# Decay rows of an mLSTM scan: broadcast by TensorE into PSUM in place of DMA and GpSimd

## The reference

```python
    def step(carry, inp):
        c_prev, n_prev, m_prev = carry
        qc, kc, vc, li, lf = inp
        b = jnp.cumsum(lf, axis=-1)
        log_d = jnp.where(tri, b[..., :, None] - b[..., None, :] + li[..., None, :], -jnp.inf)
        m_t = jnp.maximum(b + m_prev[..., None], log_d.max(-1))
        d = jnp.exp(log_d - m_t[..., None])
        inter = jnp.exp(b + m_prev[..., None] - m_t)
        s = jnp.einsum("bhtd,bhsd->bhts", qc, kc) * d
        num = jnp.einsum("bhts,bhsd->bhtd", s, vc) + inter[..., None] * jnp.einsum("bhvd,bhtd->bhtv", c_prev, qc)
        den = s.sum(-1) + inter * jnp.einsum("bhd,bhtd->bht", n_prev, qc)
        h = num / jnp.maximum(jnp.abs(den), jnp.exp(-m_t))[..., None]
        ...
        c_new = decay[..., None, None] * c_prev + jnp.einsum("bhs,bhsv,bhsd->bhvd", w, vc, kc)
```

## Time and profile before

| | before |
|---|---|
| median of 3 runs | 2023.67 us (2020.77 to 2026.71) |
| the profiled execution's own time | 2023.67 us |
| its span, first to last instruction | 2021.1 us |
| TensorE busy (matmul) | 1889.4 us, 93% |
| VectorE busy | 1170.4 us, 58% |
| ScalarE busy | 800.4 us, 40% |
| GpSimd busy | 574.2 us, 28% |
| mean granted TensorE clock | 0.965 of full speed |

### The profile page before, as it was taken

The page is one execution under the profiler, slowest core; times in us unless marked ns, Lnnn a source line. Parts: engine busy times, 40 slices in busy tenths (PEclk is TensorE's granted clock), DMA queues, the critical chain, the costliest instruction groups (busy, mean ns, idle before and its releaser), DMA issues. The chain is left out here.

```text
span 2021.1 us, 33770 instructions
## 1 busy us (share of the span) xinstructions
PE 1889.4 (93%) x7936; PEld 1340.5 (66%) x7937; DVE 1170.4 (58%) x1669; ACT 800.4 (40%) x1083; POOL 574.2 (28%) x692
## 2 busy tenths in 40 slices
PE   6999999997879899889999999999999999999785
PEld 1455458446754365478888888888888888888432
DVE  4753772203875553647538898564965873555166
ACT  0111110203230011247638888564865764555100
POOL 2000000003842220723333333332333332333244
PEclk9999996996989999999999999999999999999898
DMA  9732000001231341258648899572975892674586
GB/s 382 279 134 85 1 0 1 0 0 60 105 138 68 134 156 74 97 210 329 251 169 337 318 359 377 221 283 109 377 293 213 310 387 82 262 278 175 232 371 245
DMA packets 76095, 399.23 MB, mean 198 GB/s; under 512 B 20842, under 2 KB 21002, under 8 KB 56851
## 3 DMA queue, kind: packets, MB, share of 16 engines
q1 hardware_dynamic: 44592, 329.38, 42.2%
q0 software_dynamic: 31456, 69.27, 9.3%
q10 hardware_dynamic: 4, 0.02, 0.0%
HBM read 373.52 MB, written 73.77 MB: 221 GB/s over the span
## 5 line engine op out<-in xcount | busy, mean ns | idle before, releaser
L1708 DVE TENSOR_TENSOR split_weights<-raw_weights,split_weights (+1 forms) x384 | 448.0, 1218 | 26.6 <-ACT split_weights L671 22.9
L671 ACT ACTIVATE split_weights<-raw_weights (+1 forms) x384 | 380.9, 1063 | 9.7 <-issue 8.6
L1247 PE MATMUL psum<-split_weights,split_rows 128*128 (+1 forms) x864 | 347.8, 402 | 0.0
L1249 PE MATMUL psum<-split_weights,split_rows 128*128 (+1 forms) x864 | 337.9, 391 | 0.0
L1248 PE MATMUL psum<-split_weights,split_rows 128*128 (+1 forms) x864 | 336.6, 390 | 0.0
L671 ACT ACTIVATE arena<-psum 128x1024 f32<-128x1024 f32 (+3 forms) x202 | 164.0, 819 | 413.7 <-PE psum L1138 125.2
L671 ACT ACTIVATE split_rows<-psum 128x256 fp32r<-128x256 f32 (+1 forms) x217 | 154.2, 711 | 162.0 <-PE psum L1255 149.8
L1249 PEld LDWEIGHTS psum<-split_weights,split_rows 128*128 128x128 f32 x864 | 162.3, 188 | 35.9
L1248 PEld LDWEIGHTS psum<-split_weights,split_rows 128*128 128x128 f32 x864 | 163.0, 189 | 31.1
L1247 PEld LDWEIGHTS psum<-split_weights,split_rows 128*128 128x128 f32 x864 | 163.1, 189 | 30.1
L1266 PE MATMUL psum<-split_weights,split_rows 128*128 x432 | 168.2, 389 | 2.0 <-ACT arena L671 2.0
(11 more groups left out here) (239 smaller groups left out, 2634.1 us busy)
## 6 DMA issues: line engine op xcount, KB each, us to landing
raw_weights<-in_w_gu SPq DMA_DIRECT2D x64, 2048.0 KB
raw_weights<-in_w_dn SPq DMA_DIRECT2D x64, 1024.0 KB
arena<-pair_rows SPq DMA_DIRECT2D x16, 2048.0 KB, 13.4
arena<-in_w_ada SPq DMA_DIRECT2D x12, 2048.0 KB, 9.3
arena<-in_toks SPq DMA_DIRECT2D x18, 512.0 KB, 9.8
arena<-job_rows SPq DMA_DIRECT2D x16, 512.0 KB, 3.7
arena<-in_w_vog SPq DMA_DIRECT2D x1, 4160.0 KB, 12.7
arena<-in_w_qk SPq DMA_DIRECT2D x1, 4096.0 KB, 17.9
```

The costliest lines, as they stand in the source:

```text
L671: return act.activation(o, i, ACT.Copy)
L1247: mm(bank(3 + p), xk, part(par, 0, 512 * k), start=(k == 0), stop=False)
L1249: ins = mm(bank(3 + p), xl, part(par, 0, 512 * k), start=False, stop=(k == 7))
L1708: tt(cols(wsplit, (1 - par) * (2 * WE) + (WE + 1024 * c), 1024), cols(raw, (1 - par) * WE + 1024 * c, 1024), high, ALU.subtract).then_inc( ...
```

## The change

Ri and Rm are no longer sent through DRAM. TensorE spreads them: a product of a selector of 8 rows with a row block writes the row of one head to all 128 partitions of a PSUM bank. For Rm a product of the identity and the mask goes first into the same bank (2 or 5), in the f32r format, from a tile `maskr` that VectorE copies once. ScalarE's exponentials read that bank. VectorE multiplies q by the spread Ri straight out of bank 6, which is shared with half 1 of `update`; so TensorE writes Ri there only after the state update has read the previous half 1, and issues half 1 only after qI is made. qI is made for the current job, no longer one job ahead. `SD_done` is now given by `masks`, and ScalarE waits for it; GpSimd has no `log_decay`; VectorE no longer waits for scores apart from Dt. The rows for d = 1 are read backwards by TensorE.

```diff
-        bcast = [at(D0 + 1024 * i, 1024).rearrange("p (v h n) -> p v h n", v=2, h=4) for i in range(3)]
-        logd = at(D0 + 3072, 1024).rearrange("p (b h n) -> p b h n", b=2, h=4)
+        maskr = overlay("maskr", HB + 3600, 3 * P, F32R)
 ...
 # SP
-            sp.wait_ge(S("rows_exp"), 5)
-            sp.wait_ge(S("front_dve"), ROWS_REV_0 + 3)
-            for v, r in enumerate((Ri, Rm)):
-                for d in range(2):
-                    sp.dma_start(job_rows[d, :, DM * v:DM * v + DM]..., r[4 * d:4 * d + 4, :]...).then_inc(S("job_rows_out"), 16)
-            sp.wait_ge(S("job_rows_out"), 64)
-            def load_job(x): ...
-            for x in range(3):
-                load_job(x)
             sp.wait_ge(S("kM_evac"), NT)
             sp.dma_start(hgB, a["head_g"].to_broadcast([P, DM])).then_inc(S("hg_in"), 16)
-            for x in range(3, 16):
-                load_job(x)
             sp.wait_ge(S("SD_done"), 16)
 ...
 # GpSimd
-            def log_decay(x): ...
             for q, (s, d, t) in enumerate(JOBS):
-                if FIRSTX <= q + 1 < NJ:
-                    log_decay(q + 1 - FIRSTX)
 ...
 # ScalarE
-                act.wait_ge(S("logd_ready"), x + 1)
+                act.wait_ge(S("SD_done"), x + 1)
 ...
-                    ins = act.activation(Dt[:, x % 2, P * h:P * h + P], logd[:, x % 2, h], ACT.Exp, bias=COL[:, c0:c0 + 1])
+                    ins = act.activation(Dt[:, x % 2, P * h:P * h + P], bank(2 if x % 2 == 0 else 5)[:, P * h:P * h + P], ACT.Exp, bias=COL[:, c0:c0 + 1])
 ...
 # TensorE
-            pe.wait_ge(S("front_dve"), ROWS_REV_0 + 4)
+            pe.wait_ge(S("front_dve"), ROWS_REV_0 + 3)
 ...
+            def rows_of(r, s, d, n=P):
+                src = r[:, P * s:P * s + P]
+                return src[:, ::-1] if d else src
 ...
+            def masks(x):
+
+                s, d, t = JOBS[x + FIRSTX]
+                db = bank(2 if x % 2 == 0 else 5)
+                mm(db.rearrange("p (h n) -> p h n", h=4), maskr[:, 0:P], maskr[:, P * (1 + d):P * (2 + d)].unsqueeze(1).to_broadcast([P, 4, P]), start=True, stop=False, skip_group_check=True)
+                for h in range(4):
+                    r = 4 * d + h
+                    ins = mm(db[:, P * h:P * h + P], cst[0:8, C_SEL + P * r:C_SEL + P * r + P], rows_of(Rm, s, d), start=False, stop=(h == 3), skip_group_check=True)
                 ins.then_inc(S("SD_done"), 1)
 ...
                 if 0 <= x + 1 < 16:
                     scores(x + 1)
+                if x >= 0:
+
+                    pe.wait_ge(S("C_half"), 2 * q - 1)
+                    for h in range(4):
+                        r = 4 * d + h
+                        ins = mm(bank(6)[:, P * h:P * h + P], cst[0:8, C_SEL + P * r:C_SEL + P * r + P], rows_of(Ri, s, d), start=True, stop=True)
+                    ins.then_inc(S("I_done"), 1)
+                if 0 <= x + 1 < 16:
+                    masks(x + 1)
                 pe.wait_ge(S("vw_ready"), q + 1)
                 if q >= 1:
                     pe.wait_ge(S("C_half"), 2 * q)
                 update(q, 0, 7)
-                update(q, 1, 6)
                 if x >= 0:
                     pe.wait_ge(S("qI_ready"), x + 1)
+                update(q, 1, 6)
 ...
 # VectorE
+            for i, c0 in enumerate((C_ID, C_MF, C_MB)):
+                dve.tensor_copy(maskr[:, P * i:P * i + P], cst[:, c0:c0 + P])
 ...
-            ts(Rm, Rm, -1.0, None, ALU.mult).then_inc(S("front_dve"), 1)
+            link(ts(Rm, Rm, -1.0, None, ALU.mult))
 ...
-                dve.wait_ge(S("SD_done"), x + 1)
                 dve.wait_ge(S("D_ready"), x + 1)
 ...
-            def inter(x): ...
             for q, (s, d, t) in enumerate(JOBS):
                 x = q - FIRSTX
-                if 0 <= x + 1 < 16:
-                    inter(x + 1)
+                if x >= 0:
+                    c = t - NTC
+                    dve.wait_ge(S("I_done"), x + 1)
+                    if x >= 2:
+                        dve.wait_ge(S("N_done"), x - 1)
+                    tt(qI[:, x % 2].rearrange("p (h n) -> p h n", h=4), qkT[:, 0:4, P * c:P * c + P],
+                       bank(6).rearrange("p (h n) -> p h n", h=4), ALU.mult).then_inc(S("qI_ready"), 1)
                 if 0 <= x + 1 < 16:
                     weigh(x + 1)
```

More of the change, by code:

```diff
@@ L292, in build @@
         grow = nc.dram_tensor("modulation_rows", [4, D], F32, kind="Internal").ap()
-        job_rows = nc.dram_tensor("job_rows", [2, NT, 2 * HEADS * P], F32, kind="Internal").ap()
         def cols(t, o, n):
@@ L327, in build @@
         QTMP_READY_0, CV_EVAC_0 = 8, 16
-        MOD_READY_0, MROW_READY_0, QTMP_USED_0, CONV_DONE_0, G_EVAC_0, ROWS_EVAC_0, WARGS_READY_0, ROWS_REV_0, COLS_READY_0 = 2, 3, 7, 15, 23, 33, 39, 43, 47
+        MOD_READY_0, MROW_READY_0, QTMP_USED_0, CONV_DONE_0, G_EVAC_0, ROWS_EVAC_0, WARGS_READY_0, ROWS_REV_0, COLS_READY_0 = 2, 3, 7, 15, 23, 33, 39, 43, 46
         KM_DONE_0 = 8
@@ L383, in _ @@
             sp.dma_start(wvog, drows(a["w_vog"], 0, 1040)).then_inc(S("wvog_in"), 16)
-            sp.wait_ge(S("rows_exp"), 5)
-            sp.wait_ge(S("front_dve"), ROWS_REV_0 + 3)
-            for v, r in enumerate((Ri, Rm)):
-                for d in range(2):
-                    sp.dma_start(job_rows[d, :, DM * v:DM * v + DM].rearrange("s (h n) -> h s n", h=HEADS),
-                                 r[4 * d:4 * d + 4, :].rearrange("p (s n) -> p s n", s=NT)).then_inc(S("job_rows_out"), 16)
-            sp.wait_ge(S("job_rows_out"), 64)
[L392 to L397, removed]
-            for x in range(3):
-                load_job(x)
             sp.wait_ge(S("kM_evac"), NT)
             sp.dma_start(hgB, a["head_g"].to_broadcast([P, DM])).then_inc(S("hg_in"), 16)
-            for x in range(3, 16):
-                load_job(x)
             sp.wait_ge(S("SD_done"), 16)
@@ L1077, in scores @@
                 for h in range(4):
-                    ins = mm(bank(x % 2)[:, P * h:P * h + P], qkT[:, 4 + h, P * c:P * c + P], qkT[:, h, P * c:P * c + P], start=True, stop=True)
+                    mm(bank(x % 2)[:, P * h:P * h + P], qkT[:, 4 + h, P * c:P * c + P], qkT[:, h, P * c:P * c + P], start=True, stop=True)
+            def masks(x):
[5 more added lines that the diff above has]
+                    ins = mm(db[:, P * h:P * h + P], cst[0:8, C_SEL + P * r:C_SEL + P * r + P], rows_of(Rm, s, d), start=False, stop=(h == 3), skip_group_check=True)
                 ins.then_inc(S("SD_done"), 1)
@@ L1552, in _ @@
                 if x >= 0:
-                    c = t - NTC
                     num = psN.rearrange("p (b i n) -> p b i n", b=2, i=2)
```

## The result

The change makes the kernel slower: 2052.51 us (median of 4 runs, 2047.1 to 2056.35) against 2023.45 us (4 runs, 2020.77 to 2026.71), a ratio of 1.0138 [1.0118, 1.0157]. The forecast was 2035.2 us, and 2046 at most. The direction was right, the size was not: +29 us in place of +11.5. The profiled execution took 2050.84 us, its span is 2049.0.

A forecast was written before the change was run, and what follows sets the result against it. TensorE, busy 93% of the span, and rings with VectorE were taken as the bound; entry 3.8, steady jobs 8.9, late jobs 0.8 - 2.2 + 0.2 sum to +11.5 on 2023.67, giving 2035.2 us, range 2029 to 2046.

The forecast's parts named there:

- Steady job, 5.65 us: Eight early latent jobs: added TensorE products and half 1's wait for qI make 4.54 us into 5.65, +8.9 us.
- rival D: TensorE clock: extra work falling among steady jobs doubles issue for a few, 2 to 6 us more, 2039; chance 0.10.
- Entry, +3.8: Before the first latent job: masks(0), exponential and weighing delay the state update; first mark 507.6 for 503.78, +3.8 us.
- Late jobs, -1.2: Seven late intervals: +0.8 for the first, -2.2 for the ring of statistics without VectorE's contention, +0.2 for the last.
- the gate joining at 7.5: Late jobs: the interval in which the gate joins was taken as 7.5 us in place of 7.67.
- A: Rival: 8-row products read backwards cost double; about 2045 us, or about 2055 with all jobs at double price; chance 0.15.
- B: Rival: no change, new work fits into waits; needs a steady job below 5.0 us; 2027.6 at 4.7; chance 0.10.
- C: Rival: faster, relief of VectorE and GpSimd in the late stage decides; about 2018.7 us; chance 0.05.
- qI at 0.68 us from PSUM: VectorE's q times Ri, with one operand in PSUM, was forecast at 0.69 us.
- the wait for it as a second ring: Steady job: half 1 waiting for qI gives 5.57 us even with free 8-row products, 0.08 us below the first ring.
- the exponential under its cover: Steady job: ScalarE's exponential takes 1.26 us after masks; weighing ends 0.6 us before the next update needs it.
- w_out: Loads before the projection: start later, land at 599.5 against a projection start near 601.5; 2 us of cover, worth nothing.

The follow-up runs named there:

- dummy8: Kernel before plus eight unread 8-row products per latent job behind scores; 2036.13 us in one execution, steady jobs 5.74 to 5.75 us.
- dummy128: Kernel before plus eight unread 128-row products per latent job behind scores; 2035.07 us in one execution, steady jobs 5.36 us.
- masks_only: Kernel before with only Rm spread by TensorE (8 rows), Ri left to the transfers; 2034.62 us, ratio 1.0038, steady jobs 5.09 us.
- masks_only128: Kernel before with only Rm spread by TensorE, using 128 rows in place of 8; 2025.6 us in one run, steady jobs 4.70 us.
- adjacent: Changed kernel with the f32r mask product last, so both 8-row groups touch (two height changes, not four); 2043.71 us, ratio 1.0109.
- inter_only: Kernel before with only Ri spread by TensorE (8 rows), half 1 behind qI, masks left on GpSimd; 2037.4 us, ratio 1.0069.
- after: The changed kernel itself, 8-row products, against the kernel before; 2052.51 us, ratio 1.0138.
- rows32: Changed kernel with 32 contraction rows in place of 8, four height changes kept; 2043.07 us in one run.
- rows64: Changed kernel with 64 contraction rows in place of 8, four height changes kept; 2042.08 us in one run, later 2046.73 us.

## Why the prediction was wrong, point by point

**Steady job, 5.65 us: the first step that failed.** "So few rows buy little or nothing: I take 0.11 us per instruction" is right as to the products, 0.96 us for eight loads forwards and backwards. What had no term is the change of tile height around them. With 128 rows the job is 5.67 us and the eight jobs cost +9.0 where +8.9 was forecast; the four changes add 8 x 0.70 = 5.6. Four kernels, two by two, show it at two changes per job as well, 0.39 us (`dummy8` and `dummy128`, `masks_only` and `masks_only128`), and `adjacent` shows it within the change itself. The rows that I leaned on held a trace of it nowhere: two lone loads at the low clock. The Trainium skill has a rule that fits (TensorEngine Tiling (Array Packing), section Tiling Modes): a change of tiling mode, unlike a change of tile, drains TensorE. It gives no price. If the 8-row products count as another mode than those of 128 rows, each of the four steps waits for the products in flight, and the trace agrees, 0.2 us a step; that a drain is what the 0.2 us are, no run shows apart from their place and size. I had weighed only what the Trainium skill says of small contractions (TensorE: Matmul & The Clock Gate, section Why this matters for your kernels), that one takes as long as a product of 128 rows, and not what they cost their neighbours.

**The clock, a term put at nothing: the second step that failed.** The sum has no low clock behind 499.5; rival D had 2 to 6 us for a fall among the steady jobs. In the first profile the low clock costs some 12.8 us: 24.13 - 18.44 = 5.7 at the entry (against 64 rows, which have the same pauses), two steady jobs of 1.6 us each, and three late jobs (8.12, 8.30 and 7.82 where 7.03, 7.00 and 6.36 go at full clock), 3.9. In the second it is some 8.6: 3.0, 3.2 and 2.4. So D was right on the steady jobs (3.2 us), and had nothing for the entry and the late ones. My entry was worked out with the full clock from 499.5 on. With 64 and 128 rows the same order of work did run at full clock there; with 8 rows it was low to 510.4 in one profile and from 505 to 508.8 in the other. In the profiles few rows go with a late or a broken rise at the entry in all pairs of one order of work: 8 against 64 rows, 8 against 128. But 8 rows with two changes of height kept full clock in the steady jobs (`adjacent`, `dummy8`, `masks_only`), and 32 rows lost it in one, so rows alone do not decide. Why the clock fell, what part the pauses have in it and what part the few rows, stays open, as does the size in the timed runs.

**Entry, +3.8.** With 128 rows it is 506.31 - 488.33 - 14.38 = +3.6. The chain (`masks(0)`, exponential, weighing, state update, Ri) was right, its clock was not once the products had 8 rows.

**Late jobs, -1.2.** With 128 rows: 6.37, 6.60, 6.91, 6.99, 7.01, 6.99, 6.36 us, together 47.2 against 48.5, -1.3. The forecast had 6.3, 6.8, 7.5, three of 6.85, and 6.35. The step that is most off is the gate joining at 7.5; the sum hides it. The five middle intervals of the forecast also add up to 2.0 us less than before (34.85 against 36.85), not to the 2.2 that I wrote: the late jobs should read -1.0, and the whole sum +11.7.

**The sum.** The terms are given as +11.5; the form with 128 rows has 3.6 + 9.0 - 1.3 = +11.3 at the last mark, and 8 us in 10 timed runs. The prediction was a right sum for a kernel in which all tiles have one height. From there to the +30.8 of the changed kernel the profiles give 6.8 us for the changes of height (128 rows to 64 rows, 5.6 of it in the steady jobs) and 12.6 for the clock (64 rows to 8; 8.5 by the second profile).

**Rivals.** A's number (2045 to 2055) held the result by luck, for its mechanism did not occur: no backward product costs more. B and C fell with the steady job above 5.0 us.

**What held.** qI at 0.68 us from PSUM; the wait for it as a second ring (5.57 forecast, 5.52 in `inter_only`); the exponential under its cover (1.14 us from PSUM, less than the 1.26 taken from the earlier trace rows); w_out; TensorE waiting for no other engine between `scores` and numerator (though it lost 0.2 us at each change of height).

## What to carry to other kernels

Price small products on TensorE by what stands on either side of them: a group of few-row products among 128-row ones costs two changes of height, 0.2 us each here, besides its own time. Where the selector can be padded with zeros (and the other operand is finite there), contract over all 128 rows; where it can't, put the small products side by side. Neither made this change worth its while: even with 128 rows the kernel is 8 us slower than before, for each early job holds 2 us more of work on an engine that had 1 us free. And look at the granted clock of a stretch before adding work at its edge: a sum made at the clock of before can fail by as much as all its other errors.

## What the runs showed of the hardware

- A step between loads of 8, 32 or 64 rows and loads of 128 rows made the next load 0.2 us late at full clock (`after`, `adjacent`, `rows32`, `rows64`); within a group few rows and 128 rows both repeat every 0.11 us.
- ScalarE's exponentials of four 128x128 tiles took 1.14 us from PSUM (changed kernel) and 1.26 to 1.28 from SBUF (kernel before).
- Reading a moving operand backwards cost nothing: each steady job has one group read forwards and one backwards, and eight loads take 0.96 us in both.
- TensorE, at full clock and waiting for no other engine, was granted 1.2 GHz during part of the third and the sixth steady job of the changed kernel (0.79 over the job), in both of its profiles, and in none of the steady jobs in the two profiles of the 64-row form and the one of the 128-row form.
